# One hybrid decoder step with a mixture of experts: the last block of expert rows stays on the chip and reaches its tokens by one-hot products

## What is computed

```python
logits = (x2d @ w_router).astype(jnp.float32) + b_router
top_v, top_e = lax.top_k(logits, TOP_K)          # 4 of 32
gates = jax.nn.softmax(top_v, axis=-1)
...
def expert_block(args):
    xb, e = args
    hh = xb @ w_up[e] + b_up[e]
    return clamped_swiglu(hh) @ w_down[e] + b_down[e]
...
ys = ys * g_of_slot[:, None].astype(ys.dtype)
return jnp.zeros((T + 1, D), ys.dtype).at[tok_of_slot].add(ys)[:T]
```

## Time and profile before

| | us |
|---|---|
| median of three runs | 1437.05 |
| lowest and highest run | 1434.11, 1441.49 |
| the profiled execution | 1436.03 |
| its span, first to last instruction | 1433.9 |

### The profile page before, as it was taken

The page is one execution under the profiler, slowest core; times in us unless marked ns, Lnnn a source line. Parts: engine busy times, 40 slices in busy tenths (PEclk is TensorE's granted clock), DMA queues, the critical chain, the costliest instruction groups (busy, mean ns, idle before and its releaser), DMA issues.

```text
span 1433.9 us, 22201 instructions
## 1 busy us (share of the span) xinstructions
PE 1351.5 (94%) x6699; PEld 559.4 (39%) x6699; DVE 933.4 (65%) x2128; ACT 197.2 (14%) x380; POOL 113.2 (8%) x153
## 2 busy tenths in 40 slices
PE   8999999995898999998999999899999998999985
PEld 6865565553232333332333333233333332333322
DVE  3534246635776777786677777677777775777747
ACT  4221133321100010010100100011011010100112
POOL 3000000000010100100001000000100100001010
PEclk9999969996999999999999999999999999999997
DMA  9405110045599999999999999999999999999937
GB/s 363 103 6 176 30 40 30 31 176 228 199 402 421 421 382 423 394 421 421 421 387 405 391 420 421 420 421 376 421 390 406 413 421 421 421 383 420 393 141 288
DMA packets 82366, 460.50 MB, mean 321 GB/s; under 512 B 11838, under 2 KB 20656, under 8 KB 31924
## 3 DMA queue, kind: packets, MB, share of 16 engines
q1 hardware_dynamic: 74254, 441.43, 76.3%
q0 software_dynamic: 7520, 17.06, 3.1%
q10 hardware_dynamic: 566, 1.67, 0.3%
HBM read 623.60 MB, written 20.25 MB: 449 GB/s over the span
## 4 chain that ended last, share of the span: by engine, by line
PE 83%; DMA 9%; DVE 5%; issue 1%; ACT 1%; SPq 1%; DVEq 0%; POOLq 0%; ACTq 0%
PE ps L1711 40%; PE ps L1730 20%; DMA raw<-in_w_down_dram 7%; PE ps L1432 5%; PE ps L1409 5%; PE ps L1631 4%; PE ps L1694 2%; DMA w_a_cols<-in_w_in_dram 1%; PE ps L1592 1%; PE ps L1591 1%; DVE xT L1288 1%; PE ps L1649 1%; PE ps L1667 1%; DMA t_slots<-slot_outputs 1%; PE ps L1550 1%
## 5 line engine op out<-in xcount | busy, mean ns | idle before, releaser
L1711 PE MATMUL ps<-raw,xT 128*64 128x512 f32 x2944 | 656.5, 596 | 15.8 <-DMA raw<-in_w_up_dram 13.7
L1711 PEld LDWEIGHTS ps<-raw,xT 128*64 128x64 f32 x2944 | 205.9, 137 | 400.7 <-issue 357.6
L1288 DVE STREAM_TRANSPOSE xT<-x_hold 32x192 f32<-32x192 f32 (+1 forms) x736 | 295.1, 401 | 58.1 <-PE ps L1711 36.5
L1730 PE MATMUL ps<-raw,aT 128*64 128x512 f32 x1440 | 319.5, 593 | 8.1 <-DMA raw<-in_w_down_dram 8.1
L1288 DVE STREAM_TRANSPOSE aT<-act_g 32x256 f32<-32x256 f32 x360 | 228.5, 635 | 54.6 <-PE ps L1730 44.5
L1730 PEld LDWEIGHTS ps<-raw,aT 128*64 128x64 f32 x1440 | 102.0, 137 | 210.2 <-issue 185.8
L803 ACT ACTIVATE act_s<-act_g 128x512 f32<-128x512 f32 x46 | 29.1, 632 | 728.0 <-DVE act_g L1272 728.0
L479 POOL DMA_INDIRECT slot_outputs<-y_rows,out_idx x45 | 45.4, 1010 | 616.1 <-ACT y_rows L808 616.1
L1196 DVE TENSOR_REDUCE found<-ps 128x2 f32<-128x8 f32 x48 | 8.0, 167 | 117.3 <-PE ps L1667 117.3
L471 POOL DMA_INDIRECT x_rows<-expert_inputs,row_idx x48 | 49.4, 1029 | 362.9 <-DVE row_idx L1197 234.4
L1631 PE MATMUL ps<-w_out_sb,mixT 128*128 128x512 f32 x128 | 57.7, 605 | 2.3 <-DVE mixT L1075 2.3
(11 more groups left out here) (338 smaller groups left out, 890.3 us busy)
## 6 DMA issues: line engine op xcount, KB each, us to landing
raw<-in_w_up_dram SPq DMA_DIRECT2D x368, 1024.0 KB
raw<-in_w_down_dram SPq DMA_DIRECT2D x184, 1024.0 KB
t_slots<-slot_outputs SPq DMA_DIRECT2D x8, 1024.0 KB, 12.9
w_c_cols<-in_w_in_dram SPq DMA_DIRECT2D x1, 4096.0 KB, 31.8
w_out_sb<-in_w_out_dram SPq DMA_DIRECT2D x1, 4096.0 KB, 14.8
w_a_cols<-in_w_in_dram SPq DMA_DIRECT2D x1, 2624.0 KB, 13.1
x_sb<-in_x_prompt_dram SPq DMA_DIRECT2D x4, 512.0 KB, 5.2
w_b_cols<-in_w_in_dram SPq DMA_DIRECT2D x1, 2048.0 KB, 18.7
```

Source lines behind the costliest of these rows:

```text
L1288: dve.transpose(dst_at(rows_out, group), src_at(rows_in, parity)).then_inc(done, 1)
L1711: ins = mm(ps[SUB * i:SUB * i + SUB, bank, :], xT[:, j, :], raw[:, SLOT[j], c:c + HF], start=False, stop=(j == UPU - 1))
L1730: ins = mm(ps[SUB * i:SUB * i + SUB, 2, :], aT[:, j, r, :], raw[:, SLOT[UPU + j], D * r + HF * i:D * r + HF * i + HF], start=False, stop=( ...
```

## The change

The rows of the last block are no longer scattered and read back.

- **Slots.** Since the last block's slots are never written, `slot_outputs` is cleared once: GpSimd makes a tile of zeros of 1 KB for each partition, and ScalarE issues one DMA of 8320 rows of 1 KB on its queue in the attention stage, between `x2_rms(0)` and `move_pT(1)`. VectorE and GpSimd wait for it (`slots_cleared`) ahead of the expert loop.
- **The awaited scatter.** `blk_row` gets a second count, nb - 1, and SyncE waits for that many scatters before it loads the slots. The slots of tiles 1 to 4 go to pairs of the units of `raw` that held up weights, those of tile 0 to a tile of their own, `t_small`.
- **One-hots.** VectorE compares the positions of the last block's expert with 0 to 63 (`t_hit`), picks each token's gate for that expert (`t_gate`), and multiplies. TensorE transposes these five tiles between the third and the fourth quarter of the last down products, ScalarE copies them to `t_hitT`.
- **Products.** `t_hitT` (64 slots by tokens) times `y_last` (64 slots by 512 columns, for each half) goes into the PSUM sums of each tile behind the products of slots 2 and 3. Tile 0 has no diagonal products any more; VectorE weighs its four slots. The six products without use are gone.
- **Order.** The PSUM banks of the tiles are (0, 4, 6, 2, 0), and VectorE weighs the slots of tiles 0, 1 and 2 ahead of the first add of products.

```diff
-        R = Region(RAW0, SPL0)
-        t_slots = [R(f"t_slots{i}", [P, TOPK, D]) for i in range(NTILE)]
...
+        t_small = R("t_small", [P, TOPK, D])
+        t_shift = R("t_shift", [P, NTILE])
+        t_rank = R("t_rank", [P, NTILE, TOPK])
+        t_gate = R("t_gate", [P, NTILE])
+        t_hit = R("t_hit", [P, NTILE, 2, SUB])
+        t_hitT = R("t_hitT", [P, NTILE, P])
+        T_UNITS = [None, (0, 1), (5, 6), (9, 10), (2, 11)]
+        assert all(u in SLOT[:UPU] for pair in T_UNITS[1:] for u in pair)
+
+        def slot_pair(t, i):
+
+            return t_small[:, 2 * i:2 * i + 2, :] if t == 0 else raw[:, T_UNITS[t][i], :].rearrange("p (k n) -> p k n", k=2)
...
-            return 2 * (t % 3)
+            return (0, 4, 6, 2, 0)[t]
...
+        def scattered_blocks(e):
+            return e.value_load(blk_row[0:1, 2 * BLKS + 1:2 * BLKS + 2], min_val=NE - 1, max_val=MAXBLK - 1)
...
+            pool.wait_ge(rowp_psum, NROWP)
+            made.do(pool.memset(zeros[:], 0.0))
             pool.drain().then_inc(mixer_left, 1)
...
+            pool.wait_ge(slots_cleared, CLEARED)
             scatter(0, out_idx, y_rows)
             with pool.Fori(2, nb) as b:
                 gather(b + 2)
                 pool.wait_ge(scattered, 16 * b - 16)
                 pool.sem_inc(y_free, 1)
                 scatter(b - 1, out_idx, y_rows)
-            scatter(nb - 1, out_idx_last, y_last)
-            pool.memset(t_slots[0][0:META, :, :], 0.0).then_inc(t_cleared, 1)
+            pool.memset(t_small[0:META, :, :], 0.0).then_inc(t_cleared, 1)
...
-            sp.wait_ge(scattered, 16 * nb)
+            scattered_rows = scattered_blocks(sp)
+            sp.wait_ge(scattered, 16 * scattered_rows)
             for t, (n, first_row, token) in enumerate(parts):
                 slots = slot_dram[TOPK * token:TOPK * (token + n), :].rearrange("(p k) n -> p k n", k=TOPK)
-                sp.dma_start(t_slots[t][first_row:first_row + n, 0:2, :], slots[:, 0:2, :]).then_inc(t_loaded[t], 16)
-                sp.dma_start(t_slots[t][first_row:first_row + n, 2:4, :], slots[:, 2:4, :]).then_inc(t_rest_loaded[t], 16)
+                sp.dma_start(slot_pair(t, 0)[first_row:first_row + n], slots[:, 0:2, :]).then_inc(t_loaded[t], 16)
+                sp.dma_start(slot_pair(t, 1)[first_row:first_row + n], slots[:, 2:4, :]).then_inc(t_rest_loaded[t], 16)
...
                 x2_rms(t)
+                if t == 0:
+                    act.wait_ge(consts, NCONST + 1)
+                    act.dma_start(slot_dram.rearrange("s (h x) -> (s h) x", h=4).rearrange("(p k) x -> p k x", p=P),
+                                  bc(zeros[:], 1, [P, 4 * TOK * TOPK // P, 2 * P])).then_inc(slots_cleared, 16)
                 if t < PT:
                     move_pT(t + 1)
...
-            act.wait_ge(dn_used, DNU * nb + 2 * DNU)
-            act.activation(y_last[:], ps[:, 2, :], ACT.Copy).then_inc(y_ready, 1)
-            for t in range(NTILE):
+            for t in range(1, NTILE):
                 for k in range(2):
                     act.activation(t_diag[:, t, k, :], ident[:], ACT.Copy, scale=gates[:, t, 2 + k:3 + k]).then_inc(t_diags, 1)
+            act.wait_ge(hitT_psum, 2)
+            act.activation(t_hitT[:, 0:4, :], ps[:, 3, :].rearrange("p (t q) -> p t q", t=4), ACT.Copy).then_inc(hitT_copied, 1)
+            act.activation(t_hitT[:, 4, :], ps[:, 4, 0:P], ACT.Copy).then_inc(hitT_copied, 1)
+            act.wait_ge(dn_used, DNU * nb + 2 * DNU)
+            act.activation(y_last[:], ps[:, 2, :], ACT.Copy).then_inc(hitT_copied, 1)
...
+            step(dve.tensor_scalar(blk_row[0:1, 2 * BLKS + 1:2 * BLKS + 2], blk_cols[0:1, 3:4], -1.0, None, ALU.add))
...
+            dve.wait_ge(slots_cleared, CLEARED)
...
-            dve.tensor_copy(out_idx_last[:], out_idx_all[:, column(nb - 1)]).then_inc(out_idx_ready, 1)
+            e = expert(dve, nb - 1)
+            step(dve.tensor_scalar(t_shift[:].unsqueeze(2), pos_table[:, :, column(e)], blk_start[:, column(nb - 1)], None, ALU.subtract))
+            step(dve.tensor_tensor(t_rank[:], bc(slots_row[:, 0:2 * TOPK:2], 1, [P, NTILE, TOPK]),
+                                   slot_rank[:, :, column(e)].to_broadcast([P, NTILE, TOPK]), ALU.is_equal))
+            settle()
+            step(dve.tensor_tensor(t_hit[:], slots_row[:, 0:SUB].unsqueeze(1).unsqueeze(1).to_broadcast([P, NTILE, 2, SUB]),
+                                   t_shift[:].unsqueeze(2).unsqueeze(2).to_broadcast([P, NTILE, 2, SUB]), ALU.is_equal))
+            do(dve.tensor_tensor(t_rank[:], t_rank[:], gates[:], ALU.mult))
+            do(dve.tensor_reduce(t_gate[:], t_rank[:], AX, ALU.add))
+            dve.tensor_tensor(t_hit[:], t_hit[:], t_gate[:].unsqueeze(2).unsqueeze(2).to_broadcast([P, NTILE, 2, SUB]),
+                              ALU.mult).then_inc(hits_made, 1)
...
+            def weigh_slots(t):
+                r = rows[t]
+                x2 = t_x2[t]
                 dve.wait_ge(t_loaded[t], 16)
                 if t == 0:
                     dve.wait_ge(t_cleared, 1)
-                for k in range(2):
-                    do(dve.scalar_tensor_tensor(x2[0:r, :], y4[0:r, k, :], gates[0:r, t, k:k + 1], x2[0:r, :], ALU.mult, ALU.add))
+                    dve.wait_ge(t_rest_loaded[0], T_REST[0])
+                for k in range(TOPK if t == 0 else 2):
+                    do(dve.scalar_tensor_tensor(x2[0:r, :], slot_pair(t, k // 2)[0:r, k % 2, :], gates[0:r, t, k:k + 1], x2[0:r, :],
+                                                ALU.mult, ALU.add))
+
+            def add_products(t):
+                r = rows[t]
                 dve.wait_ge(t_pairs, t + 1)
-                do(dve.tensor_tensor(x2[0:r, :], ps[0:r, pair_bank(t):pair_bank(t) + 2, :].rearrange("p a n -> p (a n)"), x2[0:r, :], ALU.add))
+                do(dve.tensor_tensor(t_x2[t][0:r, :], ps[0:r, pair_bank(t):pair_bank(t) + 2, :].rearrange("p a n -> p (a n)"),
+                                     t_x2[t][0:r, :], ALU.add))
                 dve.sem_inc(t_summed, 1)
-                if t:
-                    last_norm(t - 1)
-            last_norm(NTILE - 1)
+
+            weigh_slots(0)
+            weigh_slots(1)
+            weigh_slots(2)
+            add_products(0)
+            weigh_slots(3)
+            add_products(1)
+            last_norm(0)
+            weigh_slots(4)
+            add_products(2)
+            last_norm(1)
+            add_products(3)
+            last_norm(2)
+            add_products(4)
+            last_norm(3)
+            last_norm(4)
...
+                    if turn_hits and j == 2:
+                        turn_hits()
+
+            def turn_hits():
+                pe.wait_ge(hits_made, 2)
+                for t in range(NTILE):
+                    r = rows[t]
+                    ins = pe.transpose(ps[:, 3 + t // 4, P * (t % 4):P * (t % 4) + r], t_hit[0:r, t].rearrange("p a s -> p (a s)"),
+                                       ident[0:r, 0:r])
+                ins.then_inc(hitT_psum, 1)
...
-            down(nb - 1, aT_last)
-            pe.wait_ge(y_ready, nb + 1)
-            for i in range(6):
-                mm(ps[:, 7, :], ident[:], xT[:].rearrange("p k q -> p (k q)"), start=True, stop=True)
-            pe.wait_ge(t_diags, 2 * NTILE)
-            pe.wait_ge(t_cleared, 1)
-            for t in range(NTILE):
+            down(nb - 1, aT_last, turn_hits)
+
+            def rest_slots(t):
                 r = rows[t]
                 pe.wait_ge(t_rest_loaded[t], T_REST[t])
-                if t >= 3:
-                    pe.wait_ge(t_summed, t - 2)
+                if t == 4:
+                    pe.wait_ge(t_summed, 1)
                 for n in range(2):
                     for k in range(2):
-                        ins = mm(ps[0:r, pair_bank(t) + n, :], t_diag[0:r, t, k, 0:r], t_slots[t][0:r, 2 + k, 512 * n:512 * n + 512],
-                                 start=(k == 0), stop=(k == 1))
+                        mm(ps[0:r, pair_bank(t) + n, :], t_diag[0:r, t, k, 0:r], slot_pair(t, 1)[0:r, k, 512 * n:512 * n + 512],
+                           start=(k == 0), stop=False)
+
+            def last_rows(t):
+                r = rows[t]
+                for n in range(2):
+                    half = slice(SUB * n, SUB * n + SUB)
+                    ins = mm(ps[0:r, pair_bank(t) + n, :], t_hitT[half, t, 0:r], y_last[half, :], start=(t == 0), stop=True)
                 ins.then_inc(t_pairs, 1)
+
+            pe.wait_ge(hitT_copied, 3)
+            pe.wait_ge(t_diags, 2 * PT)
+            rest_slots(1)
+            pe.wait_ge(hitT_copied, 4)
+            last_rows(0)
+            last_rows(1)
+            for t in range(2, NTILE):
+                rest_slots(t)
+                last_rows(t)
```

10 lines of the change are left out of this document (5 added, 5 removed).

## The result

| | before | after |
|---|---|---|
| median, us | 1437.05 | 1425.97 |
| lowest and highest run | 1434.11, 1441.49 | 1425.35, 1428.17 |
| profiled execution, and its span | 1436.03, 1433.9 | 1425.97, 1424.2 |
| issue of the last scatter from `y_rows` | 1378.93 | 1379.83 |
| from there to the end of the span | 54.97 | 44.37 |

The medians are of five executions each. The ratio is 0.9918, with an interval of 0.9904 to 0.9933: 0.8% faster. The last two lines of the table divide the span of the profiled execution: up to the last scatter of the loop (the front) it is 0.9 us longer, behind it (the **tail**) 10.6 us shorter.

What follows compares the result with a forecast made beforehand. The kernel's end was taken as bound by 8.52 MB of slot loads waiting for the last block's scatter, then VectorE. From 1436.03, -9.2 + 0.5 = -8.7 gave 1427.3, with 1.0 to the median 1428.3 us; range 1423 to 1434.

Steps and rivals of the forecast that it cites:

- The sum: Whole kernel: -9.2 us in the tail and +0.5 us in the attention stage, -8.7 us against the profiled execution.
- The wait that goes: Tail: SyncE waits for one scatter less, landing 6.8 us after issue, so slot loads start 9.1 us earlier, at 1385.7.
- The rival in which they start earlier still: Tail loads: awaited scatter lands at 1381.6 as into idle queues, 4.1 us more gain, about 1424.2; chance 0.05.
- The clock on tile 1's products: TensorE in the tail: the first full tile runs at the lower level, 1.2 GHz, taking 6.2 us; cost 1.5 us.
- the full-clock list: Tail schedule of TensorE and VectorE with full clock from the start: span's end 1423.2, a gain of 10.7 us.
- TensorE up to tile 1: Ahead of the tail's first full tile: five transposes take 1.4 us, so the down products end at 1392.1, not 1390.66.
- The named cover: TensorE: nobody waits for the later down products, since rows of y_last are needed only behind products starting at 1394.9 earliest.
- The pair of 64-row products: TensorE's products on y_last in the tail: two in different halves of the array overlap and cost 1.0 us per tile.
- Changes between the forms: TensorE in the tail: seven switches between 128-row and 64-row products cost nothing; the sum stays at 9.2 us.
- The rival that took 0.75 us for each change, or pairs that don't overlap: Tail: TensorE becomes the bound, pairs at 1.75 us each or costly switches, gain 5.5 us, about 1432.0; chance 0.18.
- The fill: Attention stage: ScalarE's clearing DMA of 8.52 MB takes 0.46 us to issue; its transfer runs 19 to 62 us.
- The front: Up to the loop's last scatter: the clearing DMA's issue ahead of the pT copies lengthens the path by 0.5 us.

Runs made afterwards that it cites:

- pairs twice: The changed kernel with the 64-row products on y_last issued twice for each tile; 1428.28 us in one run, tail 47.14 us.
- filler: The changed kernel with twelve products without use on TensorE ahead of the last down products; 1425.70 us in one run, tail 44.71 us.
- late loads: The changed kernel, but SyncE also waits for the copy of y_last before loading the slot rows; 1434.62 us, ratio 0.9985 to the kernel before.
- the same-half kernel: The changed kernel with both y_last products of each pair on partitions 0 to 63; 1429.98 us in one run, tail 47.39 us.
- the fill in two: The changed kernel with the clearing DMA cut into two of 64 partitions each on ScalarE's queue; 1444.06 us in one run.

## Why the prediction was right, and where its steps were off

The time of 1428.3 us was 2.3 too long. The sum was -8.7 against the profiled execution; that one moved by -10.06 (1436.03 to 1425.97: +0.9 in the front, -10.6 in the tail, -0.36 outside the span), which is 1.4 of it. The other 1.0 is the step from the profiled execution to the median: before, the median lay 1.0 us above, and this was carried over; after, they are the same.

- **The wait that goes**: right. The scatter landed in 6.54 us (6.8 taken), the first load went out at 1386.39, within the named 1385 to 1387, VectorE started 4.02 us behind it ("some 4 us"), and tile 1's second half came 8.97 us behind it (1394.9 - 1385.7 = 9.2 forecast). Counted from the last scatter the loads gained 9.33 us, against 9.1 plus the 0.3 by which the landing was faster. The rival in which they start earlier still had its price from a scatter into idle queues; the awaited scatter took 6.52 to 6.75 us in every profile in which the first load waits for it. That not one scatter of the loop took less than 6.4 us holds for the 200 us of the earlier trace rows alone; over the whole loop before, the shortest took 3.5 us, at the loop's start.
- **The clock on tile 1's products**: the step that failed, worth 1.5 us. The text had both lists ready, 9.2 us with the lower level and 10.7 with the full one, and took 9.2; the tail gained 10.6. By the full-clock list it ends 1423.2 - 1378.93 = 44.27 us behind the last scatter; it took 44.37. The reasons given for the lower level did not carry. The 0.50 of the earlier trace rows belongs to the down products behind 3.48 us of standing; there the fall came again and was over by 1388.5. The 0.53 over 1402 to 1404 stood behind two waits, of 2.14 us and 1.28, with the 24-row products between them:

```profile
1404.00 9.57 PE L1755 MATMUL ps<-t_slots,t_diag 128*128 128x512 f32 x16 [1.28 <-DMA t_slots<-slot_outputs]
```

  The changed kernel has neither the second wait nor those products, but one wait of 1.68 us behind the down products. Even at 2.72 us, near the 2.8 that the prediction had, the clock stayed (pairs twice); at 4.10 us (filler) and 9.53 us (late loads) it fell. An earlier fall alone does not keep the clock up: before the change it fell over the down products and at 1402 again. Which of the two, the 24-row products or the second wait, brought that fall, no run here shows. As the full-clock list was written out beside it, the time stayed within 2.3 us in spite of this step.
- **TensorE up to tile 1**: two terms were off and cancelled in part. The five transposes took 0.82 us, not 1.4. The down products took 8.05 + 1.94 = 9.99 us, not 8.53, as the lower level lasted until about 1388.5. So they ended 13.86 us behind the last scatter instead of 13.2. The named cover held: nobody waits for `y_last` before 1398.96.
- **The pair of 64-row products**: the sum was right. 1.0 us was taken; a row shows 1.13, but from tile to tile it is 4.69 us in the kernel with the filler (1406.55 to 1411.24), so the pair adds 4.69 - 3.70 = 0.99 to the row of a full tile. In the list they made TensorE the last engine by half a microsecond at the lower clock; at the full clock VectorE is last and TensorE has 0.98 us to spare.
- **Changes between the forms**: put at nothing, and that was wrong, though it did not reach the sum. Four products and a pair that lasts as long as one would be 5 x 0.85 = 4.25 us from tile to tile; it is 4.69. With both products in one half it would be 6 x 0.85 = 5.1; it is 5.54. So two changes cost 0.4 us and one about 0.2, seven of them some 1.4 us of TensorE. Single records of the same-half kernel show where: their starts lie 0.43 us apart within a form, but 0.52 at a change and 0.53 behind it; before, from tile 1's products to tile 2's in the same form, it stays at 0.43. The sum held by luck: the 3.70 us taken for each tile is the row of four products by themselves, 0.3 us more than four in a long row, and 3.70 + 1.0 came to what 3.4 + 0.85 + 0.4 comes to. That no idle time is noted ahead of a row, which was the reason given, shows nothing: none is noted here either. The rule of the Trainium skill ("TensorEngine Tiling (Array Packing)", Key Properties), that changing the tiling mode drains TensorE, agrees with these 0.2 us; the prediction kept it for a rival and left it out of the sum. The rival that took 0.75 us for each change, or pairs that don't overlap, was priced at 1432.0 with the lower clock, which is 2.5 us of it; the same-half kernel took 1429.98.
- **The fill**: 0.60 us of issue, as "about half a microsecond" had it, and 27.9 us of transfer, between the bounds of 19 and 62 but far from the 44 that was taken as the middle: a fill out of one tile at about 350 to 390 GB/s is nearer to the tail's 438 GB/s than to the transfers of the earlier trace rows. It had cover for either.
- **The front**: +0.5 was forecast and +0.9 was seen in one profile, -1.06 in the other profile of the same kernel. TensorE's marks before the fill already differ by 2.0 us at 181 us between before and after. The 0.5 as a delay of the copies of `pT` is near the 0.43 us measured on ScalarE; in the whole time it can't be told.

What stays open: in the two sessions the medians moved by 11.1 and 11.8 us (by the ratios 11.8 and 12.6), and the tail in the profiles by 10.6. The profiled execution before was 1.0 us below its median; whether the rest lies in the loop or in the tail of executions without a profile, these runs don't show.

## What to carry to other kernels

When a large transfer waits for the last of many small ones, ask which one it could do without: here the last block's rows cost 0.99 us of TensorE for each tile as products, and let 8.5 MB start 9.3 us earlier. Such an early start pays only if the consumers' order is moved with it; with the old order 3.8 of 10.6 us were lost at one add. Where a forecast hangs on a clock level, write out both lists, and look at how long TensorE will stand ahead of the step and what it did before that, not at the level the same step had before. And a row that shows no idle time ahead of it does not show that what stands there is free: compare from start to start with the same products in a long row.

## What was not expected of the hardware

- **A fill reads from half the partitions at half the rate.** Out of 128 partitions the whole fill moved at 346 to 389 GB/s in most slices, out of 64 at 190:

```profile
GB/s 0 0 0 0 0 0 156 346 349 349 261 237 387 362 386 384 389 386 387 386 378 367 358 348 354 347 324 39 0 0 0 0 0 0 0 0 13 0 0 177
```

  This is the changed kernel over 190 to 245 us, the slices as in the row of the fill in two. The 362 and 345 there are not the two halves side by side: what the slices from 209 to 217 hold above 190 is some 0.5 MB, and that is the load of the residual rows on SyncE's queue. The Trainium skill ("SBUF — State Buffer", Door 1) says that DMA bandwidth depends on how many of the 16 ports the partitions reach, and partitions 0 to 63 reach every second one; the trace agrees.
- **The next DMA of a queue can be held far longer than its issue takes**: 15.86 us behind 4.26 MB on ScalarE's queue, while SyncE's issue took 2.03 us. The same fill as a single DMA cost its engine 0.60 us. The Trainium skill ("DMA: Bandwidth & Descriptors", Issuing engines are not separate DMA queues) says that issuing on several engines saves only the time on the sequencer, which is usually small; here that time was 15.86 us. Whether the second half on SyncE's queue would have saved it, no run here shows.
- **Two products side by side in different halves of the array** last as long as one: a second pair adds 0.86 us, a product on 128 rows in a long row 0.85.
- **A change between 128-row and 64-row products costs about 0.2 us**, which no row notes as idle time: 4.69 us from tile to tile, not 4.25.
